# ScalarE rounds up to two weight panels ahead of the decays' logarithms and ahead of both directions' exponentials in the linear attention

## The reference, cut to what matters

```python
log_a = jax.nn.log_sigmoid(zz['gla_af'] @ af_w2 + af_b) / GLA_TAU      # one per direction
b = jnp.cumsum(aa, axis=2)
s_new = jnp.exp(b_last) * s + einsum(kk * jnp.exp(b_last - b), vv)
inter = einsum(qq * jnp.exp(b), s)                                      # per chunk of 64 tokens
merged = g_mla * (y_mla @ w_bm) + g_pool * (y_pool @ w_bp) + g_gla * (y_gla @ w_bg)
```

## Time and profile before

| | us |
|---|---|
| median of three runs | 1541.55 |
| the profiled execution's own time | 1542.76 |
| its span | 1541.0 |
| PE busy | 1376.8 (89%) |
| DVE busy | 846.5 (55%) |
| ACT busy | 639.2 (41%) |
| POOL busy | 733.2 (48%) |

### The profile page before, as it was taken

How to read it: one execution, slowest core, us unless ns; L and a number is a source line. 1 busy time by engine, 2 the same in 40 slices (tenths; PEclk the granted TensorE clock), 3 DMA queues, 4 the chain that set the end, 5 groups by cost and what they waited for, 6 DMA issues and landing times.

```text
span 1541.0 us, 24544 instructions
## 1 busy us (share of the span) xinstructions
PE 1376.8 (89%) x10288; PEld 1153.1 (75%) x10288; DVE 846.5 (55%) x1213; ACT 639.2 (41%) x1004; POOL 733.2 (48%) x512
## 2 busy tenths in 40 slices
PE   5798899999999999698899899978799888799997
PEld 1654688777777787383787789968688777799996
DVE  2567515431424340657577557479898644598801
ACT  3535322433322323446334554747421123555542
POOL 0520044323212644050696758738644204499983
PEclk8899999999989999799999999989899999999998
DMA  8320123244334432030334335525222134266552
GB/s 340 121 68 14 41 87 101 101 172 142 137 111 175 150 96 82 28 122 16 111 122 137 110 111 157 157 96 177 71 86 71 53 97 124 96 181 189 179 178 82
DMA packets 49118, 180.79 MB, mean 117 GB/s; under 512 B 5488, under 2 KB 6512, under 8 KB 48624
## 3 DMA queue, kind: packets, MB, share of 16 engines
q1 hardware_dynamic: 48864, 177.13, 35.6%
q10 hardware_dynamic: 144, 2.10, 0.3%
HBM read 178.16 MB, written 1.05 MB: 116 GB/s over the span
## 4 chain that ended last, share of the span: by engine, by line
PE 67%; DVE 19%; ACT 5%; DMA 4%; issue 3%; POOL 2%; SPq 0%; ACTq 0%; DVEq 0%
PE ps L368 17%; PE ps L370 16%; PE ps L369 16%; PE ps L372 16%; DMA panels<-weights 3%; DVE work L1838 2%; POOL panels_r L412 1%; ACT panels_hi L402 1%; POOL panels_r L413 1%; PE ps L959 1%; DVE work L1280 1%; DMA const_sb<-constants 1%; DVE small L1007 1%; DVE work_r L1283 1%; DVE work L802 1%
## 5 line engine op out<-in xcount | busy, mean ns | idle before, releaser
L412 POOL TENSOR_TENSOR panels_r<-panels,panels_hi 128x512 fp32r<-128x512 f32 x254 | 373.0, 1468 | 787.1 <-ACT panels_hi L402 785.7
L369 PE MATMUL ps<-h_sb_r,panels_hi 128*128 128x256 f32 (+1 forms) x1408 | 452.0, 321 | 0.0
L402 ACT ACTIVATE panels_hi<-panels 128x1024 fp32r<-128x1024 f32 x254 | 267.5, 1057 | 412.1 <-PE ps L370 236.0
L413 POOL TENSOR_TENSOR panels_r<-panels,panels_hi 128x512 fp32r<-128x512 f32 x254 | 373.4, 1470 | 0.0
L368 PE MATMUL ps<-hi_sb_r,panels_hi 128*128 128x512 f32 (+1 forms) x784 | 278.6, 355 | 27.9 <-DVE h_sb_r L683 14.0
L369 PEld LDWEIGHTS ps<-h_sb_r,panels_hi 128*128 128x128 f32 x1408 | 275.7, 196 | 17.7 <-issue 0.7
L370 PE MATMUL ps<-hi_sb_r,panels_r 128*128 128x512 f32 (+1 forms) x784 | 272.9, 348 | 0.0
L368 PE MATMUL ps<-h_sb_r,panels_hi 128*128 128x256 f32 x624 | 183.6, 294 | 12.3 <-DVE h_sb_r L664 7.6
L368 PE MATMUL ps<-work_r,panels_hi 128*128 128x256 f32 (+1 forms) x560 | 182.7, 326 | 11.7 <-POOL panels_r L413 7.6
L368 PEld LDWEIGHTS ps<-hi_sb_r,panels_hi 128*128 128x128 f32 x784 | 152.9, 195 | 53.6 <-DVE h_sb_r L683 15.3
L370 PE MATMUL ps<-h_sb_r,panels_r 128*128 128x256 f32 x624 | 178.9, 287 | 0.0
(11 more groups left out here) (325 smaller groups left out, 1814.7 us busy)
## 6 DMA issues: line engine op xcount, KB each, us to landing
panels<-weights SPq DMA_DIRECT2D x328, 512.0 KB, 3.6
x_sb<-x_in SPq DMA_DIRECT2D x1, 2048.0 KB, 8.5
x_sb<-x_in ACTq DMA_DIRECT2D x1, 2048.0 KB, 9.6
const_sb<-constants SPq DMA_DIRECT2D x1, 1216.0 KB, 11.0
out<-x_sb SPq DMA_DIRECT2D x2, 512.0 KB, 3.1
vec_sb<-vectors SPq DMA_DIRECT2D x1, 725.0 KB, 12.3
small<-c_in SPq DMA_DIRECT2D x1, 8.0 KB, 1.8
```

Of the source, the lines that this page charges most:

```text
L369: pe.matmul(o, lhsT.hi, rhs.lo, start=False, stop=False)
L402: act.activation(panels_hi[:, m:m + PANEL * P], panels[:, n:n + PANEL * P], ACT.Copy).then_inc(panel_rounded, 1)
L412: pool.tensor_tensor(panels_r[:, at:at + half], panels[:, at:at + half], panels_hi[:, m:m + half], ALU.subtract)
L413: pool.tensor_tensor(panels_r[:, at + half:at + 2 * half], panels[:, at + half:at + 2 * half], panels_hi[:, m + half:m + 2 * half], ALU.su ...
```

## The change

Three calls of `rounding.before` are added to the ScalarE program of both layers, with the point of the `gates` call that follows and at most two roundings each. No instruction is added or taken out; roundings move ahead in ScalarE's order.

```diff
                 inputs.values_scalar(act)
+                rounding.before(act, "gate", l, 0, most=2)
                 decay_logs(act)
                 gates(act, 0, GATES[l][0])
+                rounding.before(act, "gate", l, GATES[l][0], most=2)
                 exponentials(act, 0)
                 gates(act, GATES[l][0], cut[0])
...
                 gates(act, cut[2], GATES[l][1])
+                rounding.before(act, "gate", l, GATES[l][1], most=2)
                 exponentials(act, 1)
                 gates(act, GATES[l][1], cut[3])
```

## The result

The changed kernel takes 1553.57 us (median of 11 runs, 1548.59 to 1568.34) against 1542.42 (11 runs, 1538.14 to 1548.31): ratio 1.0069, 95% interval 1.005 to 1.0088. It is slower by 0.69%, where +0.55% was forecast. The median stands 0.07 us above the stated range of 1544.5 to 1553.5, but that range was built on 1541.55 us for the kernel before; 1541.55 times the ratio is 1552.2, inside it. In microseconds the interval is 7.7 to 13.6, so the forecast of +8.55 can't be told apart from the result. The profiled execution took 1557.5 us, above the median of its runs; its trace is read for the places, not for the total.

What follows compares the result with a forecast made beforehand. TensorE was taken to bound the kernel, with 67% of the chain of waits. Moved work +5.15 and clock +3.4 gave +8.55 us on the median 1541.55: 1550.1 us, range 1544.5 to 1553.5.

Steps and rivals of the forecast that it cites:

- What is emitted, and which release it waits for: Six calls: layer 0 none, 58 and 59, 79 and 80; layer 1 163, 170 and 171, 178; 163, 171, 178 wait for TensorE.
- Layer 1, logarithms: Panel 163's rounding waits for TensorE, logarithms end 3.15 later, item 2's multiply moves to 859.2: +2.5 us, bounds 1.15 to 3.15.
- The term for the interlock of the two engines' steps: In VectorE's chain after layer 1's logarithms, about 0.35 us lost in how its steps meet GpSimd's.
- Layer 1, direction 0: Panel 171's rounding waits for TensorE; `scores` starts 3.8 us later, 0.75 comes back inside: +3.05, bounds 2.6 to 3.9.
- Layer 1, direction 1: Panel 178's rounding waits until 895.90, delaying the exponentials and `scores`: +2.25 us, bounds 1.7 to 2.5.
- Layer 0: Logarithms and direction 0 cost 0; direction 1's earlier rounding shrinks TensorE's 3.1 us wait to 0.5: -2.65, bounds -3.1 to 0.
- Sum of the moved work: Both layers' moved roundings together: 2.5 + 3.05 + 2.25 - 2.65 = +5.15 us.
- The clock: 1.2 GHz stretches follow layer 1's pauses ahead of item 4 and direction 0's `scores`, 1.7 us each: +3.4, bounds 0 to 5.8.
- The rule behind the term: From 600 us on, all eleven TensorE pauses over 3.5 us have a 1.2 GHz stretch; none after 3.1 or 2.6 us.
- the one on the faster side: Early splits are what TensorE lacks: about -7 us at best, 1534.5, with both `scores` against it rather 1539.8; chance 0.05.
- the one without cost: Releases for panels 163, 171 and 178 come in time, each rounding costs ScalarE only 1.05 us: no change, 1541.5; chance 0.07.
- that the clock would not fall at the two pauses: No fall to 1.2 GHz at layer 1's two long pauses, leaving only +5.15: 1546.7 us; chance 0.20.

Runs made afterwards that it cites:

- the kernel with one rounding: Kernel before with only panel 170's rounding moved ahead of layer 1's direction-0 exponentials, panel 171's left behind them: ratio 1.0006.
- the kernel with nine and eight unread products: Changed kernel plus nine unread 512-column products ahead of item 4's wait and eight ahead of direction 0's `scores` in layer 1: ratio to before 1.0104.
- l1_logs: Kernel before with only panel 163's rounding moved ahead of layer 1's logarithms: ratio 1.0027.
- the quarter splits: Kernel before with GpSimd's split of a panel in four instructions of 128x256 instead of two of 128x512: ratio 0.993.
- the quarters' kernel with the rounding between Exp and Ln: Kernel before with four-piece GpSimd splits, layer 0's direction-1 roundings moved ahead, and panel 163's rounding between layer 1's Exp and Ln: ratio 0.9931.
- eighths: Kernel before with GpSimd's split in eight instructions of 128x128 and layer 0's direction-1 roundings moved ahead: 1594.95 us, ratio 1.0341.
- the kernel with the rounding between Exp and Ln: Kernel before with only panel 163's rounding moved, to between the Exp and the Ln of layer 1's logarithms: ratio 1.0044.

## Why the prediction was right, point by point

The mechanism was right in every place, and the term of its sum that was too small is the clock's: it counted two falls in layer 1 and put the one behind direction 1's pause at nothing.

*What is emitted, and which release it waits for*: right in all six places; the idle times of 2.13, 2.09 and 1.48 us ahead of the roundings are those foretold from SyncE's issue times (2.1, 1.8, 1.4).

*Layer 1, logarithms*, +2.5: from item 0's first gate product to item 4's the changed kernel takes 27.47 us (830.77 to 858.24) against 25.26, so +2.2. The term for the interlock of the two engines' steps (0.35 lost) was too dear; the free scan gave back the 1.0 as said.

*Layer 1, direction 0*, a pause of 3.8 and +3.05: the pause is 3.97. What comes back inside `scores` is shown by the kernel with one rounding: 1.35 us between the key turns instead of 2.1, 0.75. In the changed kernel the low clock takes part of that again (1.67).

*Layer 1, direction 1*, +2.25: the pause is 2.26. The fall of the clock behind it was in no term (below).

*Layer 0*, -2.65: the wait went from 3.15 to 0.4, so -2.7. The 6.9 us by which direction 0's exponentials move cost nothing: no wait for `decayed` appears there.

*Sum of the moved work*, +5.15: 2.2 + 3.2 + 2.3 - 2.7 = 5.0 by the traces.

*The clock*, +3.4: this is the term that was too small. Layer 1 from item 0's first gate product (830.77) to a product of 990.03 us in the kernel before (1002.62), cut at the starts of the same products in both traces:

| stretch | before, us | after, us | moved work | clock |
|---|---|---|---|---|
| item 0 to item 4 | 25.26 | 27.47 | 2.2 | 0 |
| item 4 to `scores`, direction 0 | 8.74 | 15.41 | 4.1 | 2.5 |
| `scores` and item 6's gate products | 5.46 | 6.12 | -0.75 | 1.4 |
| on to `scores`, direction 1 | 28.30 | 30.72 | 2.4 | 0 |
| on to the end | 90.36 | 92.13 | 0 | 1.75 |

From start to start a pause counts some 0.15 more than above. Of the 13.7 us in all, 5.7 are the clock: 2.5 and 1.4 behind the two pauses, near the 3.4 for these, and 1.75 behind direction 1's pause, for which the prediction had nothing. The kernel with direction 1's rounding alone shows the same: two falls there instead of one, 1.75 us longer, which with its pause makes 4.2 of its 4.9 us. In the kernel with nine and eight unread products, though, the second fall behind the same pause is missing. The stretch at half clock from 843.6 us, behind the pause ahead of item 2, costs nothing, since the wait ahead of item 4 swallows it. With layer 0's gain 13.7 - 2.7 = 11.0, near the 11.15 between the medians; that the two agree so closely is partly luck, since the rest of the changed kernel's trace differs too: falls that the kernel before has between 432 and 457 us are gone, there is one more at 703, and those at 1117 and 1198 are longer.

The rule behind the term (a fall with every pause over 3.5 us, none after 3.1 and 2.6) was drawn too sharply. In the trace of the kernel before, falls also stand beside pauses of 3.0 and 3.1 us (681.9 and 1102.6 us). With direction 0's roundings alone one follows the 2.6 us pause ahead of item 4 and costs 1.5 us, and with the logarithms' rounding alone none follows the pause of 3.4 ahead of item 2. The same pause can have a fall in one execution and none in another.

The runs list a mean clock each. Over the 74 runs of the kernel before in the experiments it is 0.9588, over the 11 of the changed one 0.9546. Within each kernel's own runs (197 in all) 0.001 of mean clock goes with 0.95 us, so 0.0042 would go with 4.0 us; the means of time differ by 11.2, which leaves 7.2 for everything else, where the traces show 5.0. These are estimates: the runs come from several chips, and the medians of the kernel before alone differ from 1540.3 to 1544.5 us between them. So how much of the 2.6 us by which the result exceeds the forecast is the clock, and how much is noise, is not settled by the times; the trace puts 2.3 of it on the clock.

*The rivals*: the one on the faster side fell with l1_logs (its best case was added up wrongly as well: 4.3, 3.1 and most of 2.6 are over 9, not 7), and would have held only where the chain is not what ends last, as with the quarter splits; the one without cost fell with the idle times; that the clock would not fall at the two pauses fell in the traces of both.

## What to carry to other kernels

An in-order engine pays for a moved instruction not only its length but the wait that moves with it: before moving one ahead of work that others wait for, look up when its release comes, for which another queue waiting on the same counter gives the time. The same move gained 2.7 us where the panel had landed, the engine was idle and TensorE stood waiting for the split, and lost 2 to 4 us where the release had not come; one rounding whose release had come, but whose split nobody waited for, made no difference to be seen (1.0006). When two engines hold each other up instruction by instruction, the size of the background engine's pieces is a knob of its own, and smaller is not always better: two, four and eight pieces gave 1, 0.993 and 1.034 (the last with layer 0's call).

## What the runs showed of the hardware that I had not expected

VectorE and GpSimd do not always take turns. In `exponents` they alternated one by one, and a step of 0.17 us took 1.2; but in the quarters' kernel with the rounding between Exp and Ln one VectorE instruction took 6.6 us longer than alone, through some nine GpSimd instructions in a row, and with eighths one took 13.6 us longer. The Trainium skill (SBUF — State Buffer, "Who interferes with whom") has the exclusive lock, and says of VectorE's two-port modes that whoever issues first gets the shared pair for the whole instruction; the traces agree for one instruction of either engine, and show beside it that the next may go to the same engine again and again. What decides between the two is open. In the kernel before no such case was found; they came with the smaller pieces.

The time lost to the clock is not settled by the sum of the pauses: the kernel before and the one with the rounding between Exp and Ln have the same pauses in all from item 0 to item 4 (25.26 and 25.35 us), but differ by 0.44%. The latter has its pauses in one piece, with a fall behind it, one more fall 20 us on, and a mean clock of 0.9539 against 0.9594 in the runs that it was compared with.
